# Six gate tiles moved into the stage of the recurrence's inputs, and the attention branch's product cut into 32 pieces inside the recurrence

## Chip, cores and metric

One core of one Trainium2 chip runs the whole program. The metric is the device time of one execution in microseconds (us); lower is better. TensorE is called PE here (PEld is its weight loads), VectorE DVE, ScalarE ACT, GpSimd POOL, and SyncE, which issues most DMAs, SP.

## The reference, cut to what matters

One decoder layer over 528 tokens (16 meta tokens and 512 of the input) of width 1024:

```python
xn = rmsnorm(h, norm1_g);  z = xn @ w_in             # columns: attention, RWKV-7, 2 x 1024 gates
y_fox  = fox_attention(q, k, v, log_f)               # causal softmax, 8 heads of 64
y_rwkv = rwkv7_time_mix(z_rwkv, ...)                 # inputs (LoRA, norms), state recurrence, group norm, bonus
gate_fox, gate_rwkv = split(sigmoid(z_gate))
mixed = gate_fox * (y_fox @ w_branch_fox) + gate_rwkv * (y_rwkv @ w_branch_rwkv)
h = h + mixed @ w_out
h = h + peer_ffn(rmsnorm(h, norm2_g), ...)           # 16384 experts, top 16 of 8 heads
```

## The kernel before, in words

The program is a row of stages. Each is a function with a `Block` in which every engine has its own instruction list; the next block starts when all engines have left the last one. The six that matter here, in order:

1. `norm_and_project` (L151) makes 27 of the 43 tiles (128 columns each) of `z`. A weight tile comes by one DMA into `wraw`, is split by ACT into a rounded `wh` (`split_hi`, L139) and by DVE into the rest `wl` (`split_lo`, L145), three slots deep, and multiplied as three fp32r matmuls per 128 rows of depth (`matmul3`, L84 to L88).
2. `fox_attention` (L415) has 32 units (head, block of 128 queries). PE's list of a unit is: two pieces of a gate tile, the transposes of the probabilities (`turn`), the scores of the unit after next, two more gate pieces, the product with the values. A gate piece is one `matmul3` over 512 columns; a tile has eight of them, so the 16 gate tiles take four pieces in each of 32 units. ACT copies a finished tile to `zG` (L499); DVE and POOL do the token shift beside it.
3. `rwkv_inputs` (L613) makes decay `L`, its exclusive form `Lx`, the rate `a`, the output gate `g`, the normed keys `kk`, `ka` and the bonus, in four blocks m of 128 channels. PE multiplies the LoRA matrices (`lora`, L741 to L752) and sums squares over heads (`head_sums`, L727). ACT does the functions, DVE a chain of dependent operations (L684 to L690).
4. `rwkv_recurrence` (L763) cuts the 528 tokens into 11 chunks of 48. `prepare` (L980) makes Gram matrices and transposes; five `level`s (L1012) invert a triangular matrix by doubling: PE multiplies (L1021, "offs", two groups g into banks 2 and 3), DVE masks (L940), PE multiplies again (L1031, "grown"), DVE adds (L949). Between the levels of chunk c stands the state update of chunk c-1 (`recur`, L1044). ACT copies the transposes out of banks 6, 7 and 0 (L886). Chunks 0, 1 and 10 are written out; chunks 2 to 9 run in a hardware loop of four turns with two chunks each (`Fori`, L846). Before each group of matmuls PE has a semaphore increment of its own (`alone`, L971). 
5. `rwkv_output` (L1071) norms the result per head (L1109, L1145, L1124, L1114, L1128, L1131, L1153 to L1156), and beside it multiplies the attention branch: eight tiles of four fp32 matmuls of 512 columns (`fox_branch`, L1101), each gated by DVE (L1142). ACT takes the sigmoids of eight gate tiles before the norm (L1121) and of eight after it (L1133).
6. `branches_and_residual` (L1162) multiplies the recurrence's branch, gates it, multiplies by `w_out` and adds the residual. Then come the second norm and the experts, which the change doesn't touch.

An fp32 matmul is two matmul records in the trace, an fp32r matmul is one.

Of the kernel before, what the change touches and what calls it, by code (L numbers as in the profile page):

```python
# [7 lines left out]

# [15 lines left out]
P = 128  # L24
# [24 lines left out]
NFIRST = len(FIRST)  # L49
WORDER = FIRST + [WZG + g for g in range(NGATE)]  # L50
# [52 lines left out]
def projection_tensors(nc, keep, ctx):  # L103
# [14 lines left out]
    sb("wl", [P, 3, KD, P], F32R)  # L118
    sb("qk", [P, NH, 2, T])
# [3 lines left out]
    keep["w_in"] = [sem(f"w_arrived{s}") for s in range(3)]  # L123
    for name in ("w_hi", "w_lo", "z_done"):
        keep[name] = sem(name)


def weight_splits(nc, d, keep):
# [19 lines left out]
    return load, split_hi, split_lo  # L148

# [265 lines left out]
def fox_attention(nc, d, keep):  # L415
# [8 lines left out]
    zT, zG, cols, yfT, qk, vtok, xh, xl, wh, wl, z_done, w_lo = (keep[n] for n in (  # L424
        "zT", "zG", "cols", "yfT", "qk", "vtok", "xh", "xl", "wh", "wl", "z_done", "w_lo"))
# [5 lines left out]
    X = slice(N_META, T)  # L431
# [5 lines left out]
    with ExitStack() as ctx:  # L437
# [3 lines left out]
        def sem(name):  # L441
# [15 lines left out]
        (steps, scores, maxed, expd, normed, turned, pt_ready, pv_done, y_out, diffed, shifted, gate_out) = (  # L457
            sem("f_" + n) for n in (
                "steps", "scores", "maxed", "expd", "normed", "turned", "pt_ready", "pv_done", "y_out", "diffed",
                "shifted", "gate_out"))  # L460
        block = ctx.enter_context(nc.Block())

        @block.sync
        def _(sp):
            for n in range(NFIRST + 3, NFIRST + NGATE):
                load(sp, n)
# [12 lines left out]
        def _(act):  # L479
# [17 lines left out]
            def gate_copy(g):  # L497
                act.wait_ge(z_done, NFIRST + g + 1)
                nc.scalar.copy(zG[:, g], g_ps[:, g % 2]).then_inc(gate_out, 1)  # L499

            exp(0)
            for u in range(NU):
                if u + 1 < NU:
                    exp(u + 1)
                pt_out(u)
                if u % 2 == 0 and u >= 2:
                    gate_copy(u // 2 - 1)
                if u % 2 == 1 and NFIRST + 2 + u // 2 < NFIRST + NGATE:
                    split_hi(act, NFIRST + 2 + u // 2)
            gate_copy(NGATE - 1)  # L510

        @block.vector
        def _(dve):
# [24 lines left out]
            for u in range(NU):  # L538
# [7 lines left out]
                if u % 2 == 1 and NFIRST + 2 + u // 2 < NFIRST + NGATE:  # L546
                    split_lo(dve, NFIRST + 2 + u // 2)
# [3 lines left out]
        def _(pe):  # L551
            def gate_product(u, ks):
                g, s = u // 2, (NFIRST + u // 2) % 3
                if ks[0] == 0:
                    pe.wait_ge(w_lo, NFIRST + g + 1)
                    if g >= 2:
                        pe.wait_ge(gate_out, g - 1)
                for k in ks:
                    mm = matmul3(nc, g_ps[:, g % 2], (wh[:, s, k], wl[:, s, k]), (xh[:, k, X], xl[:, k, X]), k == 0,
                                 k == KD - 1)  # L560
                if ks[-1] == KD - 1:
                    mm.then_inc(z_done, 1)

# [39 lines left out]
            for u in range(NU):  # L603
                k = u % 2 * 4
                gate_product(u, (k, k + 1))
                turn(u)
                if u + 2 < NU:
                    score(u + 2)
                gate_product(u, (k + 2, k + 3))
                values(u)  # L610


def rwkv_inputs(nc, d, keep):  # L613
# [3 lines left out]

    zT, cols = keep["zT"], keep["cols"]
    L, Lx, kk, ka, bonus, g = (keep[n] for n in ("L", "Lx", "kk", "ka", "bonus", "g"))
    with ExitStack() as ctx:  # L620
# [11 lines left out]
        sq = sb("r_sq", [P, 2, T])  # L632
        rk = sb("r_rk", [P, 2, T])
        rn = sb("r_rn", [P, NP4, T])
        lora_ps = ctx.enter_context(nc.psum_tensor("lora_ps", [P, 3, 2, 512], F32))
        sum_ps = ctx.enter_context(nc.psum_tensor("sum_ps", [P, 2, 512], F32))

        def squares_bank(m):

            return (sum_ps[:], lora_ps[:, 2])[m % 2][:, :, 0:TH]  # L640

        loaded = sem("r_loaded")
        squashed = sem("r_squashed")
        lora_done = sem("r_lora_done")
        lora_out = sem("r_lora_out")
        kk_raw = sem("r_kk_raw")
        squared = sem("r_squared")
        summed = sem("r_summed")
        bounded = sem("r_bounded")
        inverted = sem("r_inverted")  # L650
        rk_ready = sem("r_rk_ready")
        rk_summed = sem("r_rk_summed")
        bonus_out = sem("r_bonus_out")
        steps = sem("r_steps")
# [3 lines left out]
        def _(sp):  # L658
            sp.dma_start(wa_up[:], d["wa_up"]).then_inc(loaded, 16)
            sp.dma_start(g_up[:], d["g_up"]).then_inc(loaded, 16)  # L660
            sp.dma_start(reset[:], d["reset"]).then_inc(loaded, 16)

        @block.vector
        def _(dve):
# [4 lines left out]
            for m in range(NP4):  # L669
                dve.wait_ge(summed, m + 1)  # L670
                nc.vector.tensor_scalar(rn[:, m], squares_bank(m), 1e-24, None, ALU.max).then_inc(bounded, 1)
            link = Chain(dve, steps)
# [8 lines left out]
            for m in range(NP4):  # L681
                r, k, am = zT[:, ZR + m], zT[:, ZRK + m], a[:, m % 2]
                dve.wait_ge(lora_out, 3 * m + 3)
                link(nc.vector.tensor_scalar(Lx[:, m], L[:, m], -float(np.exp(-0.5)), None, ALU.mult))  # L684
                link(nc.vector.tensor_tensor_scan(L[:, m], reset[:], Lx[:, m], 0.0, ALU.mult, ALU.add))
                link(nc.vector.tensor_tensor(Lx[:, m], L[:, m], Lx[:, m], ALU.subtract))
# [4 lines left out]
                                               op1=ALU.mult).then_inc(rk_ready, 1)  # L691
                if m >= 1:
# [4 lines left out]
        def _(act):  # L697
            nc.scalar.activation(tanh_w[:], zT[0:HD, ZWA], ACT.Tanh).then_inc(squashed, 1)
# [1377 lines left out]
```

## Time and profile before

| | us |
|---|---|
| median of three runs (2149.43 to 2155.01) | 2152.74 |
| the profiled execution, its own time | 2154.42 |
| span of that execution, first to last instruction | 2152.6 |
| PE busy | 1979.0 (92%) |
| DVE busy | 1457.6 (68%) |
| ACT busy | 761.6 (35%) |
| mean granted TensorE clock | 0.941 |

The profile shows one execution. Busy times are shares of the span and say nothing by themselves of what a stage waits for. The granted clock of TensorE is a share of 2.4 GHz: 1.00 is 2.4 GHz, 0.50 is 1.2 GHz, a number between them is a stretch that had both. A bracket at the end of a timeline row, such as `[0.95 <-DVE off L940]`, is idle time of that engine before the row and what ended it; "issue" means nothing that the profile shows. Rows of one kind that follow each other are merged with a count.

### The profile page before, as it was taken

To read this page: it belongs to the slowest core of one execution; us is meant where nothing else is said; L and a number is where in the kernel's file an instruction comes from. 1 tells how busy PE (TensorE), PEld (TensorE's weight loads), DVE (VectorE), ACT (ScalarE), POOL (GpSimd) and SP (SyncE) were. 2 spreads that over 40 slices of the span, in tenths; PEclk is the share of its full clock that TensorE was granted. 3 is DMA by queue.
4 is the path that set the end of the run, shared out by engine and by line. 5 is a ranking of instruction groups with operands and counts; after the bars stand their busy time and mean duration, and the time that the engine had idled before them with its cause. 6 is when DMAs were issued, how large, how long until landed. Compare 5 with 4: busy or idle time off the path is not lost. (4 is left out here: it accounts for less than half of the span.)

```text
span 2152.6 us, 35660 instructions
## 1 busy us (share of the span) xinstructions
PE 1979.0 (92%) x13881; PEld 1707.8 (79%) x13881; DVE 1457.6 (68%) x3027; ACT 761.6 (35%) x1170; POOL 333.7 (16%) x317
## 2 busy tenths in 40 slices
PE   7999998687778996999999999899768999999999
PEld 6998776377666446999999999899666888888887
DVE  4243333644433415699999999899956888888887
ACT  5332334211112113333333333377623333333332
POOL 1001100000000000123322232000123222232221
PEclk9999999677876998999999999899988999999999
DMA  3222110100001205478767887428899999999997
GB/s 133 82 89 69 49 50 20 50 3 3 3 3 41 117 0 185 144 302 320 270 249 248 309 317 271 136 89 250 236 328 384 374 354 352 357 366 352 351 354 271
DMA packets 191913, 424.14 MB, mean 197 GB/s; under 512 B 16896, under 2 KB 116480, under 8 KB 190720
## 3 DMA queue, kind: packets, MB, share of 16 engines
q1 hardware_dynamic: 148832, 272.74, 36.3%
q0 software_dynamic: 39744, 144.72, 18.0%
q10 hardware_dynamic: 3168, 4.33, 0.6%
q8 instruction: 119, 1.95, 0.4%
q14 instruction: 50, 0.41, 0.1%
HBM read 367.16 MB, written 54.53 MB: 196 GB/s over the span
## 5 line engine op out<-in xcount | busy, mean ns | idle before, releaser
L86 PE MATMUL eo_ps<-vh,e_wh 128*128 128x512 f32 x768 | 300.1, 391 | 17.8 <-DVE e_wl L1899 17.7
L87 PE MATMUL eo_ps<-vh,e_wl 128*128 128x512 f32 x768 | 299.8, 390 | 0.0
L88 PE MATMUL eo_ps<-vl,e_wh 128*128 128x512 f32 x768 | 299.6, 390 | 0.0
L1512 POOL DMA_INDIRECT q_urows<-in_u_rows,gidx x112 | 136.9, 1222 | 915.0 <-DVE gidx L1608 758.0
L1849 ACT CAST vh<-vraw 128x1024 fp32r<-128x1024 f32 x128 | 134.5, 1051 | 319.5 <-PE eo_ps L88 303.1
L1890 DVE TENSOR_TENSOR vl<-vraw,vh 128x1024 fp32r<-128x1024 f32 x128 | 156.8, 1225 | 80.3 <-ACT vh L1849 79.9
L1866 POOL DMA_INDIRECT e_rows<-in_v,gidx x128 | 138.3, 1081 | 390.3 <-DVE e_acc_t L1880 351.2
L86 PE MATMUL h_ps<-x2h,h_uh 128*128 128x384 f32 x520 | 180.6, 347 | 7.0 <-DVE h_ul L1365 5.7
L86 PEld LDWEIGHTS eo_ps<-vh,e_wh 128*128 128x128 f32 x768 | 144.7, 188 | 49.1 <-DVE vl L1890 16.6
L88 PE MATMUL h_ps<-x2l,h_uh 128*128 128x384 f32 x520 | 174.7, 336 | 0.0
L87 PE MATMUL h_ps<-x2h,h_ul 128*128 128x384 f32 x520 | 174.6, 336 | 0.0
L86 PE MATMUL h_ps<-x2h,q_uh 128*128 128x384 f32 x504 | 170.0, 337 | 1.8 <-ACT h_hid L1361 1.8
L88 PE MATMUL h_ps<-x2l,q_uh 128*128 128x384 f32 x504 | 169.5, 336 | 0.0
L87 PE MATMUL h_ps<-x2h,q_ul 128*128 128x384 f32 x504 | 169.4, 336 | 0.0
L88 PEld LDWEIGHTS eo_ps<-vl,e_wh 128*128 128x128 f32 x768 | 144.7, 188 | 30.4
L87 PEld LDWEIGHTS eo_ps<-vh,e_wl 128*128 128x128 f32 x768 | 144.7, 188 | 29.9
L1880 DVE SCALAR_TENSOR_TENSOR e_acc_t<-e_rows,e_w_t,e_acc_t 128x1024 f32<-128x1024 f32 x128 | 163.8, 1279 | 3.7 <-DMA e_rows<-in_v,gidx 3.5
L1361 ACT ACTIVATE h_hid<-h_ps 128x384 f32<-128x384 f32 x128 | 63.5, 496 | 285.7 <-PE h_ps L88 184.3
L1533 DVE CUSTOM_DVE_ANT_0 q_dump<-q_urows,x2t 128x1024 f32<-128x1024 f32 x112 | 137.4, 1227 | 5.1
L147 DVE TENSOR_TENSOR wl<-wraw,wh 128x1024 fp32r<-128x1024 f32 x43 | 52.7, 1227 | 117.2 <-ACT wh L143 117.0
L86 PE MATMUL ps_z<-xh,wh 128*128 128x264 f32 x432 | 125.9, 291 | 5.7 <-DVE xl L313 5.7
L1757 PE MATMUL g_ps<-g_hot 128*128 128x128 f32 x768 | 107.0, 284 | 19.0 <-DVE g_hot L1733 18.9
(304 smaller groups left out, 4395.6 us busy)
## 6 DMA issues: line engine op xcount, KB each, us to landing
vraw<-in_v SPq DMA_DIRECT2D x128, 512.0 KB
hu_uraw<-in_u SPq DMA_DIRECT2D x63, 512.0 KB
G_scratch<-g_stage SPq DMA_DIRECT2D x24, 1024.0 KB, 11.2
gm<-G_scratch SPq DMA_DIRECT2D x128, 192.0 KB
e_hid<-HID_scratch SPq DMA_DIRECT2D x128, 192.0 KB
h_uraw<-in_u SPq DMA_DIRECT2D x45, 512.0 KB
wraw<-in_w_z SPq DMA_DIRECT2D x43, 512.0 KB, 3.3
HID_scratch<-h_hid SPq DMA_DIRECT2D x106, 192.0 KB
```

Source lines behind the costliest of these rows:

```text
L86: nc.tensor.matmul(out, a[0], b[0], start=start, stop=False)
L87: nc.tensor.matmul(out, a[1], b[0], start=False, stop=False)
L88: return nc.tensor.matmul(out, a[0], b[1], start=False, stop=stop)
L147: nc.vector.tensor_tensor(wl[:, n % 3], wraw[:, n % 3], wh[:, n % 3].bitcast(F32), ALU.subtract).then_inc(w_lo, 1)
L1361: nc.scalar.activation(hid[:, m % 2], h_ps[:, m % 2, 0:TD], ACT.Gelu).then_inc(hid_out, 1)
L1512: nc.gpsimd.indirect_dma_start(urows[:, j % GBUF_R], None, d["u_rows"], bass.IndirectOffsetOnAxis(ap=gidx[:, j:j + 1], axis=0)).then_inc(r ...
L1533: nc.vector.tensor_tensor_reduce(dump[:], urows[:, j % GBUF_R], x2t[:], 1.0, 0.0, ALU.mult, ALU.add, hdot[:, j:j + 1]).then_inc(rows_eaten, 1)
L1757: mm = nc.tensor.matmul(ps[:, n % NBANK, j], hot2[:, n % 2, j], hot1[:, n % 2, j], start=True, stop=True)
L1849: nc.scalar.copy(vh[:, c % WSLOT], vraw[:, c % VSLOT]).then_inc(v_hi, 1)
L1866: nc.gpsimd.indirect_dma_start(rows[:, j % GBUF_E], None, d["v"].rearrange("c p n -> (c p) n"), bass.IndirectOffsetOnAxis(ap=gidx[:, j:j + ...
L1880: nc.vector.scalar_tensor_tensor(out=acc_t[:], in0=rows[:, j % GBUF_E], scalar=w_t[:, j:j + 1], in1=acc_t[:], op0=ALU.mult, op1=ALU.add).t ...
L1890: nc.vector.tensor_tensor(vl[:, b], vraw[:, s], vh[:, b].bitcast(F32), ALU.subtract).then_inc(v_lo, 1)
```

## The change

- **Gates.** The attention stage computes 10 gate tiles instead of 16, spread evenly: two or three pieces in a unit instead of four, one of them ahead of the transposes. The other six tiles are computed in `rwkv_inputs`, 48 pieces between its products (`fill`), with their loads, splits and copies.
- **Inputs.** `Lx` is no longer stored: its DVE subtraction (L686) goes, and the recurrence takes the exponential of `L` one token earlier, with a column of ones in front. The LoRA products are in three parts per block, two banks are shared, squares come before the tanh and the sigmoids on ACT.
- **Recurrence.** The loop is written out for all 11 chunks, `alone` goes. "Offs" of group 1 go to bank 0 instead of bank 3, and at level 0 they wait until ACT has copied the chunk's last transposes out of bank 0. Bank 3 takes the attention branch: 32 pieces, each one fp32 matmul of 512 columns, at levels 0, 2 and 4 of a chunk, between "offs" and "grown"; after every fourth piece ACT copies the bank to `gated`. The weights `wb_fox` are loaded without waiting for the tables.
- **Output.** `fox_branch` is gone from it; ACT takes all 16 sigmoids at the end, DVE gates the eight tiles in SBUF after its chain.

The diff's core, in the order of the stages (attention; inputs with DVE, ACT and PE; recurrence; output):

```diff
+GATES_IN_FOX = 10
...
+    def product(pe, p):
+        g, k, s = p // KD, p % KD, (NFIRST + p // KD) % 3
+        if k == 0:
+            pe.wait_ge(w_lo, NFIRST + g + 1)
+            if g >= 2:
+                pe.wait_ge(gate_out, g - 1)
+        mm = matmul3(nc, g_ps[:, g % 2], (wh[:, s, k], wl[:, s, k]), (xh[:, k, X], xl[:, k, X]), k == 0, k == KD - 1)
...
             for u in range(NU):
-                k = u % 2 * 4
-                gate_product(u, (k, k + 1))
+                gate_product(pe, GATE_AT[u][0])
                 turn(u)
                 if u + 2 < NU:
                     score(u + 2)
-                gate_product(u, (k + 2, k + 3))
+                for p in GATE_AT[u][1:]:
+                    gate_product(pe, p)
                 values(u)
...
-                link(nc.vector.tensor_tensor(Lx[:, m], L[:, m], Lx[:, m], ALU.subtract))
...
+                if NFIRST + GATES_IN_FOX + 3 + m < NFIRST + NGATE:
+                    split_lo(dve, NFIRST + GATES_IN_FOX + 3 + m)
...
+            split_hi(act, NFIRST + GATES_IN_FOX + 2)
             for m in range(NP4):
                 act.wait_ge(bounded, m + 1)
                 nc.scalar.activation(rn[:, m], rn[:, m], ACT.Ln).then_inc(inverted, 1)
...
+                gate_copy(act, GATES_IN_FOX + m)
+                if NFIRST + GATES_IN_FOX + 3 + m < NFIRST + NGATE:
+                    split_hi(act, NFIRST + GATES_IN_FOX + 3 + m)
+                act.wait_ge(lora_done, 3 * m + 3)
+                nc.scalar.copy(g[:, m], w_ps[:, :, 0:TH]).then_inc(lora_out, 1)
...
+            def fill(n):
+                for p in itertools.islice(pieces, n):
+                    gate_product(pe, p)
...
+            fill(2)
             for m in range(NP4):
                 pe.wait_ge(squared, m + 1)
                 if m >= 2:
                     pe.wait_ge(bounded, m - 1)
                 head_sums(squares_bank(m), sq[:, m % 2], summed)
+                fill(1)
+            fill(2)
...
+            for m in range(NP4):
                 if m >= 1:
                     pe.wait_ge(lora_out, 3 * m)
+                lora(m, 0)
+                lora(m, 1)
+                fill(4)
+                pe.wait_ge(lora_out, 3 * m + 1)
+                lora(m, 2)
+                fill(3)
                 if m >= 1:
+                    pe.wait_ge(rk_ready, m)
+                    if m >= 2:
+                        pe.wait_ge(bonus_out, m - 1)
+                    head_sums(sum_ps[:, :, 0:TH], rk[:, (m - 1) % 2], rk_summed)
+                fill(2)
+            fill(NGATE * KD)
...
-            both(0, 0)
-            both(1, 1)
-            with eng.Fori(2, NCH - 2, 2) as c:
-                both(c, 0)
-                both(c + 1, 1)
-            both(NCH - 1, 0)
+            for c in range(NCH):
+                prepare(c, c % 2)
...
+        def fox_piece(c, slot):
+            p = c * SLOTS + slot // 2
+            return p if slot % 2 and p < KD * PIECES else None
...
             def level(c, b, lv):
...
                 for g in range(2):
                     if lv >= 1:
                         pe.wait_ge(grown_out, n * 2 + g - 1)
-                    alone()
+                    elif g == 1:
+                        pe.wait_ge(tok_out, 6 * c + 6)
                     for p, _, t in heads(range(g * HP, g * HP + HP)):
-                        mm = nc.tensor.matmul(ps[t, 2 + g, p % HP * C:p % HP * C + C], mb[t, b, p, 0:C],
+                        mm = nc.tensor.matmul(ps[t, OFF[g], p % HP * C:p % HP * C + C], mb[t, b, p, 0:C],
                                               inv[t, b, 0, p], start=True, stop=True)
                     mm.then_inc(offs, 1)
+                fox_product(c, lv + 1)
...
-            for m in range(2):
-                fox_branch(m)
...
-            for m in range(2, KD):
-                fox_branch(m)
...
-            for m in range(KD):
-                nc.scalar.activation(zG[:, m], zG[:, m], ACT.Sigmoid).then_inc(gates, 1)
             for m in range(NP4):
                 act.wait_ge(centred, m + 1)
...
-                dve.wait_ge(branch, m + 1)
-                nc.vector.tensor_tensor(gated[:, m], b_ps[:, m % 4], zG[:, m], ALU.mult).then_inc(gated_done, 1)
+                nc.vector.tensor_tensor(gated[:, m], gated[:, m], zG[:, m], ALU.mult).then_inc(gated_done, 1)
```

## Rows read from the trace of the kernel before

**Rows 1.** Busy time, granted clock and DMA of three stages.
```profile
core 0: us, PE busy (x) PEld busy (x) DVE busy (x) ACT busy (x) POOL busy (x), PEclk, DMA share, GB/s
196.60:362.00 165.40, 165.40 (x896) 123.27 (x894) 59.88 (x128) 58.85 (x158) 17.68 (x29) 1.00 0.13 42
362.00:420.00 58.00, 36.00 (x100) 18.14 (x98) 33.95 (x43) 22.41 (x30) 0.00 (x0) 0.69 0.09 28
420.00:682.00 262.00, 204.40 (x4532) 184.36 (x4532) 107.99 (x351) 43.61 (x132) 0.00 (x0) 0.72 0.03 11
```

**Rows 2.** Timeline of the attention stage: start, length, engine, line, operation.
```profile
277.46 0.25 ACT L495 COPY ptS<-pt_ps 16x128 f32<-16x128 f32 x1
...
277.62 1.04 ACT L143 CAST wh<-wraw 128x1024 fp32r<-128x1024 f32 x1
...
278.06 0.40 PE L86 MATMUL zg_ps<-xh,wh 128*128 128x512 f32 x1
...
281.03 0.39 PE L86 MATMUL zg_ps<-xh,wh 128*128 128x512 f32 x1
...
281.72 0.27 PE L585 MATMUL pt_ps<-ident,pr 128*128 128x128 f32 x1
```

**Rows 3.** Timeline of the inputs stage, PE, ACT and DVE.
```profile
374.66 0.71 PE L749 MATMUL lora_ps<-zT,g_up 128*128 128x264 f32 x2
...
375.31 0.71 PE L750 MATMUL lora_ps<-zT,g_up 32*128 32x264 f32 x2
...
379.99 0.70 ACT L719 ACTIVATE r_L<-lora_ps,cols 128x528 f32<-128x528 f32 x1
...
414.60 0.71 DVE L679 TENSOR_TENSOR r_bonus<-sum_ps,zT 128x528 f32<-128x528 f32 x1 [2.28 <-PE sum_ps L729]
```

**Rows 4.** Windows of 5 us in the inputs stage, columns as in rows 1.
```profile
385.00:390.00 5.00, 5.00 (x12) 2.41 (x12) 2.13 (x3) 1.00 (x2) 0.00 (x0) 0.50 0.00 0
```

**Rows 5.** Timeline of DVE in the recurrence, the first mask of chunks 4 to 8.
```profile
514.27 0.56 DVE L925 TENSOR_TENSOR mb<-r_ps,mgram 112x384 f32<-112x384 f32 x1 [6.37 <-PE r_ps L989]
...
533.28 0.56 DVE L925 TENSOR_TENSOR mb<-r_ps,mgram 112x384 f32<-112x384 f32 x1 [1.80 <-PE r_ps L989]
...
560.76 0.56 DVE L925 TENSOR_TENSOR mb<-r_ps,mgram 112x384 f32<-112x384 f32 x1 [7.80 <-PE r_ps L989]
...
606.68 0.56 DVE L925 TENSOR_TENSOR mb<-r_ps,mgram 112x384 f32<-112x384 f32 x1 [7.48 <-PE r_ps L989]
```

**Rows 6.** Windows of chunk 4 and chunk 9, columns as in rows 1.
```profile
514.27:533.28 19.01, 15.90 (x415) 14.54 (x413) 9.81 (x32) 3.94 (x12) 0.00 (x0) 0.86 0.01 3
...
625.80:649.64 23.84, 20.73 (x416) 18.80 (x414) 9.81 (x33) 3.94 (x12) 0.00 (x0) 0.64 0.01 2
```

**Rows 7.** Timeline of PE's weight loads in chunk 10, which is written out.
```profile
658.37 0.16 PEld L1021 LDWEIGHTS r_ps<-inv,mb 48*48 48x48 f32 x2 [1.44 <-issue]
...
664.62 0.18 PEld L1040 LDWEIGHTS r_ps<-toks 48*64 48x64 f32 x1 [1.12 <-issue]
```

**Rows 8.** Timeline of chunk 4: ACT's copies, level 0 and level 4 on PE.
```profile
517.17 2.31 ACT L886 COPY toks<-r_ps 48x256 f32<-48x256 f32 x6 [19.86 <-PE r_ps L1009]
...
518.13 0.56 PE L1021 MATMUL r_ps<-inv,mb 48*48 48x48 f32 x16
...
518.96 0.38 PE L1031 MATMUL r_ps<-off,inv 48*48 48x48 f32 x8 [0.27 <-DVE off L940]
...
530.07 0.62 PE L1031 MATMUL r_ps<-inv,off 48*48 48x48 f32 x16 [0.95 <-DVE off L940]
```

**Rows 9.** Timeline of the output stage, PE, ACT and DVE.
```profile
683.40 5.99 PE L1109 MATMUL o_ps<-yT,blockmean 128*128 128x512 f32 x8 [1.58 <-PEq L780]
...
684.65 4.27 ACT L1121 ACTIVATE zG<-zG 128x512 f32<-128x512 f32 x8
...
699.52 20.76 PE L1105 MATMUL ob_ps<-yfT,wb_fox 128*128 128x512 f32 x48
...
702.38 0.69 DVE L1153 TENSOR_TENSOR o_yc<-o_yc,o_rt 128x512 f32<-128x512 f32 x1 [5.33 <-ACT o_rt L1131]
...
720.39 0.69 DVE L1142 TENSOR_TENSOR gated<-ob_ps,zG 128x512 f32<-128x512 f32 x1 [2.74 <-PE ob_ps L1105]
```

More of the change, by code:

```diff
@@ L9 @@
+import itertools
 from contextlib import ExitStack
@@ L505, in _ @@
                 pt_out(u)
[L506 to L510, printed above, removed]
+                if u == 0:
+                    split_hi(act, NFIRST + 2)
+                for g in gates_done(u - 1) if u > 0 else ():
+                    gate_copy(act, g)
+                    split_hi(act, NFIRST + g + 3)
+            gate_copy(act, GATES_IN_FOX - 1)
         @block.vector
@@ L618, in rwkv_inputs @@
     zT, cols = keep["zT"], keep["cols"]
-    L, Lx, kk, ka, bonus, g = (keep[n] for n in ("L", "Lx", "kk", "ka", "bonus", "g"))
+    L, kk, ka, bonus, g = (keep[n] for n in ("L", "kk", "ka", "bonus", "g"))
+    rn = bonus
     with ExitStack() as ctx:
@@ L731, in head_sums, with lora @@
                 mm.then_inc(done, 1)
+            def lora(m, j):
+                c = slice(m * P, m * P + P)
+                for half in range(2):
+                    t = slice(half * TH, half * TH + TH)
+                    if j == 0:
+                        mm = nc.tensor.matmul(w_ps[:, half, 0:TH], wa_up[0:HD, c], tanh_w[:, t], start=True, stop=True)
+                    elif j == 1:
+                        mm = nc.tensor.matmul(a_ps[:, half, 0:TH], wa_up[HD:P, c], zT[HD:P, ZWA, t], start=True, stop=True)
+                    else:
+                        nc.tensor.matmul(w_ps[:, half, 0:TH], g_up[:, 0, c], zT[:, ZGD, t], start=True, stop=False)
+                        mm = nc.tensor.matmul(w_ps[:, half, 0:TH], g_up[32:64, 1, c], zT[32:64, ZFG, t], start=False,
+                                              stop=True)
+                mm.then_inc(lora_done, 1)
+            fill(2)
             for m in range(NP4):
@@ L1088, in rwkv_output @@
         ps = ctx.enter_context(nc.psum_tensor("o_ps", [P, 4, 512], F32))
-        b_ps = ctx.enter_context(nc.psum_tensor("ob_ps", [P, 4, 512], F32))
-        mean, centred, squared, var, rooted, steps, loaded, gates, branch, gated_done = (sem("o_" + n) for n in (
-            "mean", "centred", "squared", "var", "rooted", "steps", "loaded", "gates", "branch", "gated"))
+        mean, centred, squared, var, rooted, steps, loaded, gates, gated_done = (sem("o_" + n) for n in (
+            "mean", "centred", "squared", "var", "rooted", "steps", "loaded", "gates", "gated"))
         block = ctx.enter_context(nc.Block())
@@ L1131, in _ @@
                 nc.scalar.activation(rt[:, m], rt[:, m], ACT.Exp, scale=-0.5).then_inc(rooted, 1)
-            for m in range(KD):
-                nc.scalar.activation(zG[:, KD + m], zG[:, KD + m], ACT.Sigmoid).then_inc(gates, 1)
+            for m in range(NGATE):
+                nc.scalar.activation(zG[:, m], zG[:, m], ACT.Sigmoid).then_inc(gates, 1)
         @block.vector
@@ L1146, in _ @@
             dve.wait_ge(centred, NP4)
-            for m in range(2):
-                gate(m)
             for m in range(NP4):
@@ L1156, in _ @@
                 link(nc.vector.tensor_tensor(yrT[:, m], yc[:, m], g[:, m, X], ALU.mult))
-                gate(2 + m)
-            for m in range(2 + NP4, KD):
+            for m in range(KD):
                 gate(m)
```

287 lines of the change are left out of this document (131 added, 156 removed).

## The prediction, made before the changed kernel was run

> **What bounds the kernel now.** I read the windows by stage first, then the timelines inside the four stages that the change touches. The windows say where an engine is full [rows 1]: in the attention stage PE is busy 165.4 of 165.4 us at a clock of 1.00 and DVE only 59.9, so a matmul taken out of it shortens it by its own length. In the inputs stage nothing is full (PE 36 of 58, DVE 34), the clock is 0.69: a chain through ACT, PE and DVE. The recurrence is also a chain (PE 204 of 262, clock 0.72). The output stage ends on PE again: DVE's last gate waits 2.74 us for the attention branch's product [rows 9]. So the question is what moved work costs where it lands.
>
> **Attention stage.** One gate piece goes by in 281.72 - 281.03 = 0.69 us at 2.4 GHz [rows 2]. Six tiles of eight pieces leave: 48 x 0.69 = -33 us. The ends of this term: the cover can be gone. The values product waits for ACT's copies of the transposes, which in a unit of the longest kind end at 277.46 + 0.25 = 277.71, and the first gate piece after the scores ends at 278.06 [rows 2]; one piece there is enough, and no unit has fewer. Splits and copies become fewer on ACT and DVE, and each of these has under 2 us of work (59.9 and 58.9 over 32 units [rows 1]) in a unit that shrinks from about 5.2 to 4.1. I keep -33; if every second unit stalled by 0.3 us it would be -28.
>
> **Inputs stage.** Now it ends with the bonus at 414.60 + 0.71 = 415.3 [rows 3]. PE's list after, at 2.4 GHz: an fp32 matmul of 264 columns takes 375.31 - 374.66 = 0.65 us [rows 3]. Before the LoRA blocks: eight pieces (5.6) and eight head sums of some 0.5 (4.2), so PE is there at about 363.5 + 10 = 373.5. The first LoRA products take about 2.0 (the two 64-row kinds no longer alternate, I count three of four), four pieces 2.8: 378.3. Then PE waits for the first sigmoid `L`. That one stands at 379.99 now [rows 3]; ACT gets a weight split of 1.04 [rows 2] in front of it, and waits for squares a bit differently, so about 381.5. From there PE is full: the rest of block 0 is 2.6 + 3.5 = 6.1, the other three blocks cost 2.0 + 2.6 + 1.1 for head sums + 9 x 0.69 and restarts = 12.1 each, four last pieces 2.9, the last sums and the bonus 1.8. The end is 381.5 + 6.1 + 36.3 + 2.9 + 1.8 = 428.6, +13.3 us. DVE's chain hides: it loses the subtraction of 0.71 per block and gets a split of 1.2, some 5 us in a block of 12. ACT's too. The loads of four weight tiles lie behind three small ones on SP's queue; they land long before their splits. The 3 us in which PE stands still may drop the clock, and I add 2. Sum +15. The bounds: +13, and a case far above that is a rival below.
>
> **Recurrence, the loop.** At a loop turn PE stands still: DVE's first mask waits 6.37, 7.80 and 7.48 us against 1.80 in a chunk without a turn [rows 5]. That is (6.37 + 7.80 + 7.48) - 3 x 1.80 = 16.3 us that go with the loop. But written-out code has its own stops: in chunk 10 PE waits 1.44 and 1.12 us for nothing the profile shows [rows 7], and I find shorter ones inside the loop too. Between nothing and 8 x 2.56 = 20 us comes back. The pieces of the attention branch are long matmuls with few instructions, in which the stream can catch up; I take +2. The Trainium skill (Runtime: NRT & Kernel Launch, Instruction fetch mechanics) says that a taken branch breaks the sequential prefetch and forces a fetch, and that fetching straight code is hidden. By it the sum would have 0 here in place of +2. The first half agrees with the loop turns above, the second is against the stops of chunk 10.
>
> **Recurrence, the new wait and the pieces.** At level 0 "offs" start at 518.13 and "grown" at 518.96 [rows 8]. Now group 1 must wait for ACT's six copies, which end at 517.17 + 2.31 = 519.48 [rows 8]. Then 0.25 us of "offs", then the piece. A piece is two of the 48 records that take 20.76 us [rows 9]: 0.86 us at 2.4 GHz, 1.7 at 1.2. "Grown" starts at about 519.5 + 0.25 + 0.86 = 520.6, so +1.6 us per chunk. Queued behind the waiting "offs" on PE is the whole rest of the level, and DVE and ACT wait for it. At level 2 the piece fills a gap of about 0.35 and costs +0.5. At level 4 there is a gap of 0.95, since DVE is busy with the state [rows 8], and the piece costs nothing at 2.4 GHz and +0.7 at 1.2. Over 11 chunks: 17.9 + 5.5 + 0 = +23. The bounds: 19 (if the copies come a bit earlier) and 23 + 22 x 0.86 + 7 = 49 with every piece at 1.2 GHz. I take 23, since the clock stood at 2.4 in most of levels 0 to 2. The removed increments on PE: DVE to PE takes 0.1 us with them, nothing to win that I can see; -2 to 0, I take 0. ACT's eight copies of the bank (0.6 each) lie where it is idle, 19.86 us before its copies [rows 8].
>
> **Recurrence, the clock.** A chunk with the clock at 0.86 takes 19.0 us, one at 0.64 takes 23.8 [rows 6]. Chunks 4 to 9 without their two loop turns average (649.64 - 514.27 - 6.0 - 5.7) / 6 = 20.6 us [rows 5, 6], 1.6 above chunk 4, so 11 x 1.6 = 18 us hang on the clock in the middle of the chunks. The pieces put work into the gaps, the new wait makes one of 1.1 us. I take half, -9; the bounds are -18 and 0. The recurrence in sum: -16.3 + 2 + 23 - 9 = 0.
>
> **Output stage.** The squares no longer wait for eight sigmoids of 4.27 us [rows 9], nor the variance sums for the eight fp32 matmuls of the first two tiles. With the last mean at 683.40 + 5.99 = 689.4 [rows 9] and centred by 690.1, squares follow at once, the variances end near 693, logarithms 693.5, exponentials from 695: DVE's chain starts at about 695.5 in place of 702.38 [rows 9]. Sixteen operations, 10.8 us, to 706.3; eight gates at 0.72, 5.8 us, to 712.1. Now the end is 720.39 + 0.69 = 721.1 [rows 9]: -9. The sigmoids end at some 707 and are hidden. But PE has been idle for 19 us when the next stage starts, where it was at 2.4 GHz until now. The stage's own start shows the price: eight records took 5.99 us that take 3.4 at full clock [rows 9], +2.6. Sum -6.4.
>
> **The sum.** -33 + 15 + 0 - 6.4 = -24.4 us on the profiled execution's 2154.4 gives 2130.0. It stood 1.7 above the median of the runs, so 2128.3, call it 2128, 1.1% faster. A measurement of this kernel can tell about 0.3% (6.5 us) from no change.
>
> **Rivals.**
> 1. *The clock stays up in the recurrence.* For it: chunk 4 held 2.4 GHz from its third microsecond to its end, with three small gaps, two of which the pieces fill. Against it: the wait of 1.1 us per chunk, and the idle time at each chunk's end. It gives the other 9 us of the clock's term. And chunk 4 still ran 0.28 x 19 = 5.3 us at 1.2 GHz (clock 0.86), which is worth up to 2.6 per chunk; a quarter of that, 8 us, is counted: 2128 - 17 = 2111. Chance 0.25.
> 2. *The written-out chunks run as the slow ones do, with the pieces on top (slower).* The place is the middle of each chunk: a fetch stop or the new wait lowers the clock, and each chunk takes 23.8 [rows 6] + 2.1 + 0.9 for a piece at 1.2 GHz = 26.8 in place of a mean of (649.64 - 514.27) / 6 = 22.6 with turns. That is 8 x 4.2 = +34, and +5 for the other three. 2128 + 39 = 2167. It decides against the change from +25 us in the recurrence on, about 25 us per chunk. For it: chunk 9 with its clock of 0.64 [rows 6] and the stops of chunk 10 [rows 7]. Against it: long matmuls give the stream time. Chance 0.09, and 0.21 for the ground between this and the forecast (2134 to 2158), of which 0.12 lies within 0.3%.
> 3. *The inputs stage runs at 1.2 GHz.* From 385 to 390 PE was busy 5.00 of 5.00 us and the clock was 0.50 [rows 4]. If it stays so with the gate pieces between, 47 us of PE's list double: 2128 + 45 = 2173. Against it: gate pieces alone held 1.00 through the whole attention stage [rows 1]. Chance 0.03.
> 4. *The forecast*, chance 0.42. That the change does not do what it says I see no place for: the counts of pieces are plain.
>
> Range: the forecast, rival 1 and most of the ground above: 2106 to 2152. Faster by over 0.3%: 0.42 + 0.25 + 0.09 = 0.76; within: 0.12; slower: 0.12.
>
> **What would show each step.** The attention stage should be about 132 us long with PE still full. In the inputs stage PE should be busy without a gap after the first `L`, at a clock near 1, and the stage some 15 us longer. In the recurrence the waits of 6 to 8 us before L925 should be gone, "offs" of group 1 at level 0 should wait for ACT's copies, and a chunk should take some 22.5 us at a clock of 0.75 to 0.8. The output stage should be about 29 us. I am wrong if a chunk takes under 20.5 or over 25 us, or if the inputs stage shows half clock.

## Result and the profile after

| | before | after |
|---|---|---|
| median of four runs, us | 2153.88 | 2096.36 (2093.83 to 2099.73) |
| the profiled execution, its own time | 2154.42 | 2095.05 |
| mean granted TensorE clock | 0.941 | 0.971 |

The ratio is 0.9732, with a 95% interval of 0.9704 to 0.9761: 2.7% faster, where 2128 was forecast and 2106 was the lower end of the range. The profiled executions differ by 59.4 us. To see where they lie I cut both traces at the first instruction of each stage. The last row is the expert stages, which the change doesn't touch, and the lead-in.

| stage, us | before | after | difference | forecast |
|---|---|---|---|---|
| attention | 167.9 | 143.8 | -24.2 | -33 |
| inputs | 52.0 | 66.2 | +14.2 | +15 |
| recurrence | 267.8 | 228.2 | -39.6 | 0 |
| output | 38.0 | 29.8 | -8.2 | -9 |
| branches | 86.5 | 88.0 | +1.5 | +2.6 |
| rest | 1540.4 | 1537.2 | -3.2 | 0 |

So the forecast failed in one stage, by 40 us, and in another by 9 the other way. The windows of the four stages and of one chunk, of after (columns as in [rows 1], which cut the same stages less sharply, and [rows 6] for the chunk):

```profile
194.25:338.01 143.76, 135.75 (x760) 96.55 (x760) 57.15 (x125) 52.93 (x148) 19.45 (x30) 1.00 0.11 34
338.01:404.22 66.21, 60.45 (x240) 42.37 (x240) 31.86 (x41) 28.19 (x38) 0.00 (x0) 0.92 0.14 48
404.22:632.41 228.19, 191.45 (x4596) 151.84 (x4596) 111.97 (x355) 49.80 (x142) 0.00 (x0) 0.95 0.04 14
632.41:662.25 29.84, 9.84 (x16) 4.03 (x16) 18.14 (x28) 19.73 (x31) 0.00 (x0) 0.61 0.18 70
488.33:507.65 19.32, 16.81 (x424) 13.29 (x421) 9.75 (x32) 3.94 (x12) 0.00 (x0) 1.00 0.01 3
```

The recurrence went from a clock of 0.72 [rows 1] to 0.95. A chunk takes 19.32 us at 1.00, where chunks of 19.0 and 23.8 us stood before [rows 6]. DVE's first masks, the counterpart of [rows 5], now come every 19.32 to 19.34 us from the second chunk on:

```profile
469.00 0.56 DVE L971 TENSOR_TENSOR mb<-r_ps,mgram 112x384 f32<-112x384 f32 x1 [1.00 <-PE r_ps L1043]
488.33 0.56 DVE L971 TENSOR_TENSOR mb<-r_ps,mgram 112x384 f32<-112x384 f32 x1 [1.00 <-PE r_ps L1043]
507.65 0.56 DVE L971 TENSOR_TENSOR mb<-r_ps,mgram 112x384 f32<-112x384 f32 x1 [1.00 <-PE r_ps L1043]
526.99 0.56 DVE L971 TENSOR_TENSOR mb<-r_ps,mgram 112x384 f32<-112x384 f32 x1 [1.00 <-PE r_ps L1043]
```

Level 0 of one chunk, in the timeline of after, the counterpart of [rows 8]:

```profile
470.57 2.31 ACT L930 COPY toks<-r_ps 48x256 f32<-48x256 f32 x6 [9.79 <-PE r_ps L1061]
...
471.53 0.38 PE L1075 MATMUL r_ps<-inv,mb 48*48 48x48 f32 x8
...
472.94 0.38 PE L1075 MATMUL r_ps<-inv,mb 48*48 48x48 f32 x8 [1.03 <-ACT toks L930]
473.25 1.12 PE L1030 MATMUL r_ps<-yfT,wb_fox 128*128 128x512 f32 x2
...
474.30 0.38 PE L1085 MATMUL r_ps<-off,inv 48*48 48x48 f32 x8
```

The wait for ACT's copies is there, 1.03 us, the piece stands behind it, and the next products follow at once. From "offs" to "grown" it takes 474.30 - 471.53 = 2.77 us, before 0.83 [rows 8]. The stops of [rows 7] are gone: nowhere in the written-out recurrence of after does PE stop for over 0.55 us for nothing that the profile shows.

The other stages, in the timeline of after: a transpose of the attention stage, the first `L` and PE behind it in the inputs stage, DVE's chain and gates in the output stage, and the first product of the stage behind it.

```profile
317.10 0.66 PE L610 MATMUL pt_ps<-ident,pr 128*128 128x128 f32 x4 [0.90 <-DVE pr L560]
...
355.45 0.70 ACT L741 ACTIVATE r_L<-lora_w_ps,cols 128x528 f32<-128x528 f32 x1
356.20 1.25 PE L780 MATMUL lora_w_ps<-zT,g_up 128*128 128x264 f32 x2 [4.55 <-ACT r_L L741]
...
364.91 0.40 PE L88 MATMUL zg_ps<-xh,wh 128*128 128x512 f32 x1
...
646.04 0.69 DVE L1186 TENSOR_TENSOR o_yc<-o_yc,o_rt 128x512 f32<-128x512 f32 x1 [6.44 <-ACT o_rt L1167]
...
657.08 4.91 DVE L1177 TENSOR_TENSOR gated<-gated,zG 128x512 f32<-128x512 f32 x8
...
662.30 9.87 PE L1237 MATMUL b_ps<-zT,wb_rwkv 128*128 128x512 f32 x19 [19.99 <-PEq L1128]
```

### The profile page after: what moved, and what is told of

It is laid out like the page before. It is cut to its first block and busy times, and to the rows that moved or that the text cites. A ratio compares the mean times of both kernels' runs of the same rounds, so it can differ in the third digit from the quotient of the medians.

```text
span 2093.2 us, 34968 instructions
## 1 busy us (share of the span) xinstructions
PE 1933.1 (92%) x13881; PEld 1660.6 (79%) x13881; DVE 1454.6 (69%) x3024; ACT 767.1 (37%) x1177; POOL 336.9 (16%) x317
## 5 line engine op out<-in xcount | busy, mean ns | idle before, releaser
L90 PEld LDWEIGHTS eo_ps<-vl,e_wh 128*128 128x128 f32 x768 | 144.8, 189 | 30.3
L1803 ACT COPY g_stage<-g_ps 128x512 f32<-128x512 f32 x96 | 103.3, 1078 | 57.0 <-PE g_ps L1789 57.0
```

The lines of the kernel that those rows point to most:

```text
L90: return nc.tensor.matmul(out, a[0], b[1], start=False, stop=stop)
L1803: nc.scalar.copy(stage[:, tile % 2, :, i * TB:i * TB + TB].rearrange("p a t -> p t a"), ps[:, n % NBANK]).then_inc(staged, 1)
```

## Experiments

The change does five things in the recurrence at once: the loop is written out, the increments go, `Lx` goes, a wait comes, pieces come. The first three runs begin to part them.

**e1: only the loop written out.**

```diff
-            both(0, 0)
-            both(1, 1)
-            with eng.Fori(2, NCH - 2, 2) as c:
-                both(c, 0)
-                both(c + 1, 1)
-            both(NCH - 1, 0)
+            for c in range(NCH):
+                both(c, c % 2)
```

> The kernel before with the recurrence's loop written out and nothing else. Its recurrence stage took 267.8 us, the changed kernel's 228.2. Theory A (the long pieces of the attention branch hold the clock at 2.4 GHz): only the three loop turns go, 16 us, the stops of PE for instructions come back in part, so the stage takes 250 to 262 us at a clock of 0.70 to 0.80, and the run 2136 to 2148. Theory B (writing out alone holds the clock, since nothing stops PE long enough): the clock is above 0.95 and the stage takes 205 to 215 us, the run about 2095.

Measured: 2133.56 us; the recurrence takes 249.5 us at a clock of 0.75, so writing it out is worth 18.2 us, and the stops are there. PE in the timeline of e1, within one chunk:

```profile
486.17 0.38 PE L1027 MATMUL r_ps<-off,inv 48*48 48x48 f32 x8 [0.27 <-DVE off L936]
...
492.01 0.29 PE L1017 MATMUL r_ps<-inv,mb 48*48 48x48 f32 x4 [1.39 <-issue]
...
496.60 0.33 PE L1017 MATMUL r_ps<-inv,mb 48*48 48x48 f32 x5 [0.73 <-issue]
```

The second row stops in the middle of a level's "offs", after 12 of their 16 records and so inside the second group of eight, behind no wait. Over the stage I add up 11.3 us of such stops in 14 places.

**e2: the loop kept, with 33 pieces, the bank 0 and the wait.** The pieces' results aren't used.

```diff
+    OFF = (2, 0)
...
+                    elif g == 1:
+                        pe.wait_ge(tok_out, c * 6 + 6)
                     alone()
...
+                if lv in (0, 2, 4):
...
+                    nc.tensor.matmul(ps[:, 3], keep["wb_fox"][:, 0, 0:P], keep["yfT"][:, 0], start=True, stop=True)
                 for g in range(2):
                     pe.wait_ge(off_out, n * 2 + g + 1)
```

> The kernel before, its loop kept, with 33 matmuls of 512 columns at levels 0, 2 and 4, group 1 of the offs in bank 0 and the wait for ACT's copies; the products are of one fixed tile and nobody reads them, the branch is still multiplied in the output stage. Theory A: the clock is 1.00 in the chunks except for some us behind each loop turn, a chunk without a turn takes about 19.5 us, the stage about 19.3 x 11 + 16 = 245 us, the run about 2132. Theory B: the clock stays near 0.72, each chunk becomes longer by the pieces and the wait (+2 to +4 us), the stage takes 290 to 310, the run 2175 to 2195.

Measured: 2158.31 us, recurrence 277.0 us, clock 0.89. The pieces do hold the clock up (0.72 to 0.89), but the stage is 9.2 us longer, which lies between the two expectations (245, and 290 to 310). With loop and increments in place the pieces and the wait pay back a part of their own time and no more.

**e3: after, with the attention branch back in the output stage,** the loop written out, the wait kept.

```diff
-            return p if slot % 2 and p < KD * PIECES else None
+            return None
...
+            for m in range(2):
+                fox_branch(m)
...
+            for m in range(2, KD):
+                fox_branch(m)
```

> The changed kernel without the 32 pieces: the attention branch is multiplied in the output stage as before. The wait for ACT's copies at level 0 stays. Theory A: the clock falls to 0.7 to 0.8 and PE stops for instructions one or two times per chunk; a chunk takes 21 to 24 us, the stage 245 to 260 in place of 228.2, the run 2120 to 2135. Theory B: the clock stays above 0.95, a chunk takes 19.33 - 0.86 - 0.5 = about 18 us, the stage 213 us, and with the output stage 8 us longer the run takes about 2088.

Measured: 2094.21 us, recurrence 220.7 us at 0.87, output 38.7. The gain is there without the pieces. Their move is a draw: +7.5 us in the recurrence, -8.8 in the output, +1.5 in the branches. So the 28.8 us of the recurrence between e1 (249.5) and e3 (220.7) lie in what e3 has and e1 hasn't: no increments and no `Lx`. The wait, which e3 also has and e1 hasn't, is priced by e7.

**e4: twelve gate tiles in the attention stage instead of ten.**

```diff
-GATES_IN_FOX = 10
+GATES_IN_FOX = 12
```

> The changed kernel with 12 gate tiles in the attention stage and four in the inputs stage. Theory C (the attention stage at 10 tiles is bound by the chain of scores, maximum, exponential and norm: PE idles for 7 us before the transposes): 16 pieces more cost it less than their 11.1 us, 2 to 6, and the inputs stage, where PE is full from the first L on, gives back 11; the run is 5 to 9 us faster than the changed kernel, about 2089. Theory D (PE's list bounds the attention stage still): +11 and -11, no difference.

Measured: 2094.82 us, 0.9727 [0.9681, 0.9773] of before, no difference from after. Attention 151.8 (+8.05), inputs 58.0 (-8.24). A piece is worth 0.50 to 0.52 us in either place.

**e5: e1 without PE's increments.** Nothing waits for this semaphore.

```diff
             def alone():
-                pe.sem_inc(passed, 1)
+                return
```

> The kernel before with the recurrence's loop written out, as in e1, and PE's increments of the otherwise unused semaphore (some 20 a chunk, ahead of each group of products) taken away; no pieces, no new wait, Lx kept. Recurrence stage in e1: 249.5 us, clock 0.75, with stops of PE of 0.7 to 1.4 us for nothing that the profile shows. Theory A (the increments break PE's stream of instructions, and the stops pull the clock down): those stops are gone, the clock is 0.85 or more, the stage takes 215 to 225 us, the whole about 2105. Theory B (something else in the change does it: the wait that groups PE's work, or the shifted exponentials that came with Lx's removal): the stage stays at 245 to 252 us, the stops stay, the whole is about 2133.

Measured: 2097.94 us, recurrence 214.3 us. This edit and the loop alone come to the change's own total: what the change gains in the other stages (16.7 us by the table above) its wait and its pieces cost in the recurrence (13.9), and the rest is within the spread of the runs. The windows of the recurrence, of e1 and then of e5:

```profile
413.25:662.78 249.53, 201.34 (x4532) 182.48 (x4532) 112.69 (x354) 45.16 (x134) 0.00 (x0) 0.75 0.04 13
```

```profile
415.38:629.67 214.29, 177.23 (x4532) 158.38 (x4532) 111.53 (x354) 45.15 (x134) 0.00 (x0) 0.84 0.05 15
```

The same 4532 matmuls. PE's idle time falls from 249.5 - 201.3 = 48.2 to 37.1 us, by about as much as the stops (11.3 to 0.4). Its busy time falls by 24.1, because more of it runs at 2.4 GHz. That the stops pull the clock down isn't shown: in windows of half a microsecond the clock falls to 1.2 GHz eleven times in e1 and eleven times in e5, which has a single stop of 0.40 us. What differs is how long it stays there, 3 to 17 us in e1 and 3 to 7 in e5 (the last fall of each, which lasts to the end of the stage, left out).

An experiment given without a range or an interval is a single execution. Two pairs of kernels with the same recurrence show how well one execution gives a stage: after and e4 with 228.2 and 227.9, e8 and e12 with 217.1 and 217.0.

**e6: after with the increments put back.**

```diff
                     elif g == 1:
                         pe.wait_ge(tok_out, 6 * c + 6)
+                    alone()
...
                     pe.wait_ge(off_out, n * 2 + g + 1)
+                    alone()
...
```

> The kernel after with PE's increments of an otherwise unused semaphore put back ahead of each group of products, everything else as after (stage 228.2 us, clock 0.95, no stops). Theory A: stops of PE of 0.7 to 1.4 us come back, the clock falls to 0.8 or less, the stage takes 245 to 260 us and the whole about 2115 to 2125. Theory B: 226 to 231 us, the whole about 2096. Between: the stops come back but the pieces hold the clock up, 233 to 243 us.

Measured: 2139.48 us, recurrence 273.8 us at 0.83, 45.6 more than after: 13.6 of them idle time of PE, 32.0 busy time. The edit works from both sides, and more strongly than either theory said; the pieces don't shield from it. PE in the timeline of e6:

```profile
496.76 0.26 PE L1103 MATMUL r_ps<-ar,ST 64*64 64x48 f32 x2 [0.88 <-issue]
...
506.88 0.28 PE L1053 MATMUL r_ps<-ar,kt 64*48 64x96 f32 x2 [1.11 <-issue]
```

**e9: e1 with each increment ahead of its wait.** The same instructions, two of them in the other order.

```diff
...
+                    alone()
                     pe.wait_ge(off_out, n * 2 + g + 1)
-                    alone()
...
```

> As e1 (the kernel before, loop written out, 28 increments a chunk kept), but each increment stands ahead of the wait of its group and not between the wait and its first product: the same instructions in number, only the order of two changed. e1: recurrence stage 249.5 us, stops of PE of 0.7 to 1.4 us; e5 without the increments: 214.3, none. Theory S (separation: an increment behind a wait keeps the wait apart from the matmul, PE's sequencer itself stands at the wait, takes in nothing meanwhile, and afterwards runs dry): the stage falls to 214 to 225 us and the stops go. Theory N (number or kind: any 28 more instructions that write a semaphore between the products do it): it stays at 240 to 255 us with the stops.

Measured: 2098.15 us, recurrence 218.8 us at 0.83, one stop of 1.17 us left early in the stage and one of 0.39 at its end. All 28 increments a chunk are still there (26 of them belong to a wait), and they cost 4.5 us against e5 where they cost 35.2 in e1. So it is not their number.

**e10: e1 with 8 of the 28 increments,** those outside the levels.

```diff
...
                         pe.wait_ge(grown_out, n * 2 + g - 1)
-                    alone()
...
                     pe.wait_ge(off_out, n * 2 + g + 1)
-                    alone()
```

> As e1, with the 20 increments a chunk of the levels taken away and the 8 a chunk of the preparation and of the state's products kept. If the price goes by number, 8/28 of the 35.2 us between e1 and e5 stay: 224 us in the stage. If it is the levels' short groups of 8 or 16 products alone, about 214 to 217. If it is a threshold that few increments already pass (the stream falls behind once), 235 to 250.

Measured: 2099.05 us, recurrence 215.8 us. The eight cost 1.5 us, where 8/28 of 35.2 would be 10; taking the 20 out of the levels gives back the rest. Whether it is their place in the levels' short groups that counts, or that eight a chunk are few enough anywhere, this run doesn't tell.

**e13: e1 with two increments behind each wait.**

```diff
                 pe.sem_inc(passed, 1)
+                pe.sem_inc(passed, 1)
```

> As e1 (loop written out, one increment behind each wait, stage 249.5 us), with two increments behind each wait. Theory S (the wait is torn off its matmul, the number does not matter): 248 to 256 us in the stage, about the same stops. Theory N (each instruction between costs, 35.2 us for 28 a chunk): about 285 us, total about 2168.

Measured: 2137.63 us, recurrence 250.9 us. The second increment costs nothing in sum. What one or two of them do at a single wait can be read from PE's idle time behind DVE's `off`. The rows are of e5, of e9 and of e13; e1's 0.27 stands above:

```profile
480.58 0.38 PE L1027 MATMUL r_ps<-off,inv 48*48 48x48 f32 x8 [0.18 <-DVE off L936]
```

```profile
481.35 0.38 PE L1027 MATMUL r_ps<-off,inv 48*48 48x48 f32 x8 [0.18 <-DVE off L936]
```

```profile
491.10 0.38 PE L1028 MATMUL r_ps<-off,inv 48*48 48x48 f32 x8 [0.42 <-DVE off L936]
...
500.78 0.26 PE L1037 MATMUL r_ps<-mb,nu 48*64 48x48 f32 x3 [1.40 <-issue]
```

0.18, 0.27 and 0.42 us for none, one and two behind the wait, and 0.18 with one ahead of it; within 0.01 these are also the commonest values of each stage. The time behind the wait grows with each, the stage doesn't. The stops for nothing that the profile shows are fewer in e13 than in e1, 6.0 us in 11 places, so they and the waits together make up the idle time, 49.0 us for e1's 48.2. What counts in the order of e1, e9 and e13 is whether the wait stands on another instruction than the matmul.

What this fits is how the Trainium skill (Perfetto Trace Analysis, Per-engine timelines) draws the two kinds: a matmul goes with its wait into a queue, and the sequencer takes in the next instruction meanwhile; an instruction of the sequencer alone holds it until its semaphore is there. By that rule an increment behind a wait takes over the wait, and PE comes out of it with nothing taken in; one ahead of the wait doesn't. e9 and e13 are what it would give. That an increment is such an instruction of the sequencer, and that the stops are late instructions, no row shows; the stops stand under "issue".

**The other five** belong to the wait, the pieces and the attention stage.

**e7: e3 without the wait,** "offs" of group 1 in bank 3 again.

```diff
-    OFF = (2, 0)
+    OFF = (2, 3)
...
-                    elif g == 1:
-                        pe.wait_ge(tok_out, 6 * c + 6)
```

> As e3 (after, with the attention branch back in the output stage), and also the second group's offs in the bank of before, so that PE doesn't wait for ACT's copies at level 0. e3: recurrence stage 220.7 us, clock 0.87, total 2094. The wait and what is behind it on PE was priced at 1.1 us a chunk (11 chunks): if it is on the path the stage takes about 208 to 210 us and the whole 2082. If the copies set the pace anyway through a later wait (the chain through the tokens), or the clock falls without it, the stage stays at 218 to 222 and the whole at 2094.

Measured: 2089.86 us, 0.9703 [0.9674, 0.9732]; recurrence 213.9 at 0.85. The wait costs 6.8 us, 0.62 a chunk, less than the 1.03 that PE stands at it in after; the clock is a little lower without it, and what else takes the rest is open. And 213.9 is e5's 214.3: the shifted exponentials, and whatever else e7's recurrence has and e5's hasn't, are worth nothing that these two traces show.

**e8: after, with the level-0 piece inside the wait.**

```diff
                     elif g == 1:
+                        fox_product(c, 1)
                         pe.wait_ge(tok_out, 6 * c + 6)
...
-                fox_product(c, lv + 1)
+                if lv:
+                    fox_product(c, lv + 1)
```

> The kernel after with the level-0 piece of each chunk put between the offs of the first group and PE's wait for ACT's copies, where PE stands still for about 1.03 us. If the price of the wait and the piece is simply their sum on the path (1.0 + 0.86 us less what overlaps), some 0.8 us of each chunk go: the stage 219 to 220 us for 228.2, the whole about 2087, a ratio of 0.969 to before. If the path at level 0 runs through DVE or ACT instead, nothing changes: 228 and 2096.

Measured: 2085.09 us (2083.2 to 2087.94), 0.9685 [0.9654, 0.9715]; recurrence 217.1 at 0.95. PE in the timeline of e8, with no idle time left around the piece:

```profile
469.44 0.38 PE L1076 MATMUL r_ps<-inv,mb 48*48 48x48 f32 x8
469.76 1.13 PE L1030 MATMUL r_ps<-yfT,wb_fox 128*128 128x512 f32 x2
...
470.85 0.38 PE L1076 MATMUL r_ps<-inv,mb 48*48 48x48 f32 x8
```

1.0 us a chunk is gained, a little more than the 0.8 expected: wait and piece stood one behind the other on the path.

**e11: e8, and the level-2 piece ahead of each chunk's first product,** where PE waits for DVE.

```diff
-            p = c * SLOTS + slot // 2
-            return p if slot % 2 and p < KD * PIECES else None
+            at = (1, 3, 5) if c == 0 else (0, 1, 5)
+            if slot not in at:
+                return None
+            p = c * SLOTS + at.index(slot)
+            return p if p < KD * PIECES else None
...
             def prepare(c, b):
+                fox_product(c, 0)
                 pe.wait_ge(scaled, 4 * c + 3)
...
-                fox_product(c, 0)
```

> As e8 (piece of level 0 in the wait; stage 217.1, total 2085.1), and the level-2 piece of each chunk but the first put ahead of the chunk's first product, where PE waits 0.9 us for DVE's scaled operands. If the pieces only fill idle time there, 10 x about 0.6 us go: the stage 210 to 212, total 2079. If the piece holds up the first product (PE reaches that place late) or waits for ACT's copy of the bank: 215 to 220, total 2083 to 2088.

Measured: 2091.24 us, 0.9696 [0.9669, 0.9722]; recurrence 223.7 at 0.91, slower than e8 by the total. The windows of three chunks in a row, and what stands in the second (of e11):

```profile
485.81:503.39 17.58, 16.85 (x424) 13.28 (x421) 9.75 (x33) 3.93 (x12) 0.00 (x0) 1.00 0.02 3
503.39:530.81 27.42, 25.47 (x424) 20.24 (x420) 10.13 (x33) 4.51 (x13) 0.00 (x0) 0.63 0.01 2
530.81:548.38 17.57, 16.83 (x424) 13.26 (x420) 9.75 (x32) 4.52 (x13) 0.00 (x0) 1.00 0.01 3
```

```profile
504.94 2.31 ACT L933 COPY toks<-r_ps 48x256 f32<-48x256 f32 x6 [9.68 <-PE r_ps L1065]
...
507.28 0.58 ACT L926 COPY gated<-r_ps 128x512 f32<-128x512 f32 x1
507.91 1.12 PE L1033 MATMUL r_ps<-yfT,wb_fox 128*128 128x512 f32 x2 [1.62 <-ACT gated L926]
```

Seven of ten chunks are as hoped, 17.3 to 17.8 us for e8's 18.3. But in three of them the piece ahead of the chunk finishes a tile, and the next piece waits until ACT, busy with its six copies, has emptied the bank: 1.62 us. After two of these waits the clock stayed at 1.00 and the chunks took 19.2 us; after the one at 507.91 the clock fell within 2 us, and the chunk took 27.4 us.

**e14: e11 with ACT's copy of the tile ahead of its six copies.**

```diff
             def prepare(c, b):
+                fox_copy(c, 0)
                 for j, bank in enumerate((6, 7, 0)):
...
-                fox_copy(c, 0)
```

> As e11, with ACT's copy of a finished tile of the branch ahead of its six copies of the transposes in the three chunks where the piece ahead of the chunk finishes a tile; in e11 PE waited 1.62 us for that copy, and one of these chunks went on at 1.2 GHz and took 27.4 us. If that wait started the slow stretch: all chunks at 17.6 to 17.8 us, clock 1.00 in the middle of the stage, stage 209 to 213 us, total 2078 to 2081. If the slow stretch comes without it too (piece ahead of the chunk as such): stage 218 to 225, total about 2090.

Measured: 2079.02 us (2076.67 to 2083.32), 0.9656 [0.9641, 0.9671] of before: the best kernel here, 3.4% faster than before where the change is 2.7%. The recurrence takes 210.8 us. The same place as above in the timeline of e14, without a wait, and DVE's first masks of that chunk and the next, 17.58 apart:

```profile
506.05 1.13 PE L1033 MATMUL r_ps<-yfT,wb_fox 128*128 128x512 f32 x2
```

```profile
503.21 0.56 DVE L974 TENSOR_TENSOR mb<-r_ps,mgram 112x384 f32<-112x384 f32 x1 [1.09 <-PE r_ps L1047]
520.79 0.56 DVE L974 TENSOR_TENSOR mb<-r_ps,mgram 112x384 f32<-112x384 f32 x1 [1.09 <-PE r_ps L1047]
```

**e12: e8 with two gate pieces ahead of the transposes.**

```diff
-                gate_product(pe, GATE_AT[u][0])
+                for p in GATE_AT[u][:2]:
+                    gate_product(pe, p)
...
-                for p in GATE_AT[u][1:]:
+                for p in GATE_AT[u][2:]:
```

> As e8, and in the attention stage the second gate piece of each unit is put ahead of the transposes too, which wait up to 2 us for DVE's normed scores in 11 of 32 units. Attention stage in e8: 143.7 us, of which PE is idle 8.0. If one more piece of 0.6 us covers part of that wait: 138 to 141 us, total about 2081. If the later scores only push DVE's maxima back by as much: 143 to 146, total 2085.

Measured: 2086.18 us, 0.9669 [0.9644, 0.9694], the same as e8; attention stage 144.8. The piece takes the waits for the norm from 7.0 only to 6.2 us and uncovers 2.2 us of waits for ACT's copies, in the timeline of e12:

```profile
318.79 0.65 PE L610 MATMUL pt_ps<-ident,pr 128*128 128x128 f32 x4 [0.69 <-DVE pr L560]
333.20 1.23 PE L622 MATMUL pv_ps<-ptS,vtok 128*64 128x128 f32 x8 [0.71 <-ACT ptS L533]
```

The kernel before with its loop kept and the increments taken away was not tried. So what they cost inside the loop is open; the 18.2 and 35.2 us hold for this order of the two edits.

## Why the prediction was wrong

By its own steps, with what each term measured. The sign of being wrong was a chunk under 20.5 us, and it takes 19.32. For the recurrence the runs give a chain from before to after: 267.8, written out 249.5 (e1), no increments 214.3 (e5), no `Lx` 213.9 (e7), wait 220.7 (e3), pieces 228.2 (after). Each link is one edit but that of `Lx`, which holds all that e7 and e5 differ in.

- **The removed increments: the step that failed.** "DVE to PE takes 0.1 us with them, nothing to win that I can see; -2 to 0, I take 0." They were worth -35.2 us with the loop written out (e1 to e5). I priced them as instructions on the path, by their own length. Even so read, [rows 8] showed 0.27 us between DVE and PE, and I had no row without them beside it: 0.18 (e5). The larger part lies elsewhere: from e1 to e5 PE's idle time falls by 11.1 us, about what the stops come to, and its busy time by 24.1 at a higher clock. The bound from the trace should have come from the stops: they stood in the rows, I had no cause for them, and the only instructions in PE's list that compute nothing were these. A removed instruction whose purpose is unclear, 28 times a chunk, deserved a range like that of the stops, and a rival of its own.
- **The loop.** -16.3 and +2 for stops that come back, -14.3 in sum; measured -18.2 with the increments still there. The +2 was taken from the stops of [rows 7]. Once the increments are gone those stops are, too (0.4 us left in e5). So the rule of the Trainium skill that I set aside (Runtime: NRT & Kernel Launch, Instruction fetch mechanics: fetching straight code is hidden) does agree with the runs, for a list whose waits stand on the matmuls; that the stops of the others are fetches no row shows.
- **The wait, the pieces and the clock.** +23 - 9 = +14; measured +6.8 + 7.5 = +14.3. That the sum is right is luck, since the parts weren't: the wait is 0.62 us a chunk, not 1.1, and the pieces 0.68 net of what they bring in clock (0.87 without, 0.95 with). By rival 1 the clock stays up in the recurrence. It did, and more so than there (1.00 between 420 and 620 us), but half of the way from 0.72 to 0.95 isn't the pieces' doing: with the loop and the increments gone the clock is at 0.84 with no piece at all (e5).
- **Attention.** -33, with a bound at -28; measured -24.2. PE's busy time falls by 166.9 - 135.8 = 31.2, so a piece is 0.65 us and not 0.69, and its idle time grows from 1.0 to 8.0. That is the stall that I named and put at nothing: I looked at the cover of the values product, where it held, and not at the transposes, which wait for DVE's normed scores, while DVE itself waits for PE's scores (41.5 us, 26.1 before). A shorter unit leaves less time from the one to the other; that this is what uncovers the wait is my reading of the two waits. The groups of the attention stage in after:

```profile
L554 DVE TENSOR_REDUCE nmx<-s_ps 128x1 f32<-128x144 f32 (+3 forms) x32 | 16.2, 505 | 41.5 <-PE s_ps L600 41.5
...
L610 PE MATMUL pt_ps<-ident,pr 128*128 128x128 f32 x80 | 14.5, 280 | 7.0 <-DVE pr L560 7.0
```

  e4 and e12 show that neither fewer moved tiles nor one more piece in front gains it back.
- **Inputs.** +15, measured +14.2. The first `L` starts 17.4 us into the stage and 16.4 before (I had +1.5), PE stands still for 4.55 us until it is done, has half the clock until 364.91, and 1.00 after that. So rival 3, half the clock through the stage, did not come.
- **Output and branches.** -9 and +2.6, measured -8.2 and +1.5. DVE's chain starts 13.6 us into the stage (12.1 forecast), and ends 29.6 into it (28.7). The first 19 records of the next stage take 9.87 us, before 8.39.
- **Rival 2**, slow chunks at 1.2 GHz, which would have made it slower, fell with the stops that it rested on. But e11 has one chunk of 27.4 us, near its 26.8, behind another wait.

Adding up: -24.4 forecast, -35.2 for the increments, -3.9 for the loop, +8.8 for the attention stage, and small ones: -0.8 inputs, +0.8 output, -1.1 branches, +0.3 wait and pieces, -0.4 `Lx`, -3.2 in stages that weren't touched. That is -59.1 of the measured -59.4.

## What to carry to other kernels

Look at what each wait of PE stands on. With a wait on an instruction of its own, even one that computes nothing, a list of many short matmuls ran 35 us (1.7% of the program) slower than without these instructions, and 31 us slower than with each of them moved ahead of its wait. A moved piece of work belongs into an idle time that is there in every turn, and whoever must empty its bank has to be free by then: e11 and e14 differ by one line and 12 us.

## Unexpected in the hardware

- The position of one instruction against a wait: 28 increments a chunk cost about 35 us behind the waits (e1), 36.6 with twice as many (e13), and 4.5 ahead of them (e9), all against e5 and from a single execution each.
- One wait of PE of 1.62 us can be followed by some 20 us at 1.2 GHz: a chunk of 27.4 us at a mean clock of 0.63 (e11), which is (1 - 0.63) x 2 x 27.4. The same wait at 435.70 and at 588.31 of the same execution left the clock at 1.00 and its chunk at 19.2 us, so it is a risk and not a fixed price.
- At a clock that stays up, the pieces' 36.0 us of PE's busy time (64 records in e8) cost 3.2 us in the recurrence, e8's 217.1 against e7's 213.9, and e7 has no wait for the copies.
